# Down weights of the middle experts asked for by ScalarE, behind its copy of the down result, on a queue of their own

## The reference

```
x = x + gt_a * (concat(retention(h), mlstm(h)) @ w_out)
h2 = rms_norm(x, g_ffn) * (1 + sc_f) + sh_f
logits = h2 @ w_router + b_router             # 32 experts, top 4 of each token
expert e:  hu = xe @ w_up[e] + b_up[e]         # w_up[e] is 1024 x 2048
           gate = min(hu[:, :1024], 7);  lin = clip(hu[:, 1024:], -7, 7)
           y = ((lin + 1) * gate * sigmoid(1.702 * gate)) @ w_down[e] + b_down[e]   # 1024 x 1024
x = x + gt_f * (sum over the 4 experts of a token, by its softmax weight)
y = rms_norm(x, g_final)
```

## Time and profile before

| | before |
|---|---|
| median of three runs | 1326.92 us |
| the profiled execution | 1324.58 us, span 1322.8 us |
| TensorE busy (PE) | 1189.2 us, 90% of the span |
| ScalarE busy (ACT) | 176.3 us, 13% |
| read from memory | 459.66 MB, 352 GB/s over the span |
| packets of queue 1 | 461.75 MB, 85.8% of the 16 engines' span |
| packets of queue 10 | 4.37 MB, 1.1% |

### The profile page before, as it was taken

How to read it: one execution, slowest core, us unless ns; L and a number is a source line. 1 busy time by engine, 2 the same in 40 slices (tenths; PEclk the granted TensorE clock), 3 DMA queues, 4 the chain that set the end, 5 groups by cost and what they waited for, 6 DMA issues and landing times.

```text
span 1322.8 us, 23572 instructions
## 1 busy us (share of the span) xinstructions
PE 1189.2 (90%) x8761; PEld 556.1 (42%) x8764; DVE 387.1 (29%) x857; ACT 176.3 (13%) x334; POOL 71.6 (5%) x180
## 2 busy tenths in 40 slices
PE   5999999898989999998999988999877989988996
PEld 4655447645534344443334432444222334333332
DVE  0173215737331221231222121132211221222225
ACT  3002231012101001010111100011110000110101
POOL 1010001323000000000000000000000000000001
PEclk9999999988989999998999998999988999989998
DMA  9934634784569999999999999999999999999992
GB/s 371 358 129 177 225 128 192 223 322 145 235 238 404 396 415 410 422 421 423 421 422 422 422 422 422 422 387 423 423 422 422 422 421 423 420 422 422 423 421 89
DMA packets 80911, 467.22 MB, mean 353 GB/s; under 512 B 8714, under 2 KB 26958, under 8 KB 28778
## 3 DMA queue, kind: packets, MB, share of 16 engines
q1 hardware_dynamic: 78202, 461.75, 85.8%
q10 hardware_dynamic: 2288, 4.37, 1.1%
q0 software_dynamic: 384, 0.59, 0.2%
HBM read 459.66 MB, written 6.42 MB: 352 GB/s over the span
## 4 chain that ended last, share of the span: by engine, by line
PE 65%; DMA 20%; SPq 8%; DVE 3%; issue 3%; POOL 0%; ACT 0%; POOLq 0%; DVEq 0%
PE psum L998 18%; DMA mem<-in_w_up 18%; PE psum L1036 12%; PE psum L1046 8%; SPq L417 7%; PE psum L650 6%; PE psum L965 4%; PE psum L631 3%; PE psum L837 2%; DMA mem<-in_mod_chunks 2%; PE psum L654 2%; PE psum L506 1%; PE psum L758 1%; PE psum L1054 1%; PE psum L1002 1%
## 5 line engine op out<-in xcount | busy, mean ns | idle before, releaser
L998 PE MATMUL psum<-mem 128*32 128x512 f32 (+2 forms) x2432 | 404.3, 626 | 83.8 <-DMA mem<-in_w_up 61.4
L998 PEld LDWEIGHTS psum<-mem 128*32 128x32 f32 (+2 forms) x2432 | 122.2, 122 | 357.5 <-issue 215.8
L1036 PE MATMUL psum<-mem 128*32 128x512 f32 (+3 forms) x1024 | 213.0, 598 | 0.0
L2066 DVE TENSOR_SCALAR mem<-psum 128x256 f32<-128x256 f32 (+3 forms) x32 | 19.2, 601 | 554.8 <-PE psum L1002 554.8
L1046 PE MATMUL psum<-mem 128*128 128x512 f32 (+1 forms) x384 | 152.2, 607 | 2.0 <-issue 1.5
L2087 DVE TENSOR_TENSOR mem<-mem,psum 128x1024 f32<-128x1024 f32 (+1 forms) x96 | 100.3, 1045 | 97.7 <-PE psum L1046 97.7
L1036 PEld LDWEIGHTS psum<-mem 128*32 128x32 f32 (+3 forms) x1024 | 79.6, 128 | 106.2 <-issue 100.0
L965 PEld LDWEIGHTS psum<-mem 128*128 128x128 bf16 x2304 | 77.5, 99 | 20.4 <-issue 20.1
L650 PE MATMUL psum<-mem 128*128 128x512 f32 x192 | 84.2, 595 | 0.0
L965 PE MATMUL psum<-mem 128*128 128x64 bf16 (+1 forms) x2304 | 81.3, 197 | 0.0
L1392 ACT ACTIVATE mem<-mem 128x256 f32<-128x256 f32 (+3 forms) x32 | 17.9, 559 | 465.7 <-DVE mem L2066 465.7
(11 more groups left out here) (275 smaller groups left out, 820.0 us busy)
## 6 DMA issues: line engine op xcount, KB each, us to landing
mem<-in_w_up SPq DMA_DIRECT2D x256, 1024.0 KB, 22.9
mem<-in_w_down SPq DMA_DIRECT2D x128, 1024.0 KB, 17.9
mem<-in_mod_chunks SPq DMA_DIRECT2D x12, 2048.0 KB, 12.2
mem<-in_in_chunks SPq DMA_DIRECT2D x8, 2048.0 KB, 9.8
mem<-in_out_chunks SPq DMA_DIRECT2D x2, 2048.0 KB, 10.0
mem<-in_x_prompt ACTq DMA_DIRECT2D x2, 1024.0 KB, 6.4
mem<-in_state_ret SPq DMA_DIRECT2D x4, 512.0 KB, 8.6
mem<-in_state_mlstm_c SPq DMA_DIRECT2D x4, 512.0 KB, 7.8
```

What stands on the lines that cost most here:

```text
L998: last = pe.matmul(out, xg[:, c, cols], moving, start=(c == 0), stop=False)
L1036: last[c] = pe.matmul(psum[slots * q:slots * q + slots, 6 + u, :], turned, piece_slot(home + c, 2, D)[:, piece % 2, 512 * u:512 * u + 512] ...
```

## The change

SyncE no longer asks for the down pieces of experts 1 to 30. ScalarE does, at the end of its iteration e, for the down pieces of expert e, after it has issued the copy of the down result of expert e-1. It needs no wait of its own for the places, since its copy of the turned activations (L1409) already waits for all four `piece_done`. The down pieces of expert 0 and of the last expert stay with SyncE. The branch for blocks over 128 tokens is changed likewise; it doesn't run with these inputs.

```
-            def load_downs(e, it):
-
-                for c in range(DOWN):
-                    sp.wait_ge(piece_done[UP + c], it)
-                    load_down(e, c)
-
...
             with sp.Fori(2, NE) as e:
                 load_ups(e, e)
-                load_downs(e - 1, e - 1)
             sp.wait_ge(S("counts_ready"), 1)
...
+            def load_downs(e):
+
+                for c in range(DOWN):
+                    src = a["w_down"][0][e, 256 * c:256 * c + 256, :].rearrange("(p h) n -> p h n", h=2)
+                    act.dma_start(piece_slot(UP + c, 2, D), src).then_inc(piece_in[UP + c], 16)
+
...
             with act.Fori(1, NE) as e:
                 expert(0, e, e, count_at(e + 1), count_at(e + 2))
+                with act.If(e < NE - 1):
+                    load_downs(e)
+                with act.Else():
+                    act.nop()
```

More of the change, by code:

```diff
@@ L466, in _ @@
                 with sp.Fori(1, ROUNDS) as r:
-                    load_ups(0, r * NE)
-                    load_downs(NE - 1, r * NE - 1)
-                    with sp.Fori(1, NE) as e:
+                    with sp.Fori(0, NE) as e:
                         load_ups(e, r * NE + e)
-                        load_downs(e - 1, r * NE + e - 1)
                 load_last(NE * ROUNDS)
@@ L1458, in _ @@
                 with act.Fori(1, ROUNDS) as r:
+                    load_downs(NE - 1)
                     copy_gathered(r * (NE + 1), None)
```

## The result

| | before | after |
|---|---|---|
| median | 1327.07 us (4 runs, 1325.17 to 1330.02) | 1361.51 us (4 runs, 1354.69 to 1367.36) |
| ratio, 95% interval | | 1.0255 [1.0212, 1.0298] |
| profiled execution, span | 1324.58, 1322.8 us | 1364.28, 1362.4 us |

The account below looks back on a forecast made before the run. The DMA engines were taken to bound the expert loop. Late asks 22 us plus end order 6 us gave 28 us, which on the profiled 1324.6 us made 1352 us, range 1335 to 1374.

Parts of the forecast that it names:

- SyncE's removed asks 0: Expert loop: SyncE's standing at L422 until the down was done held nothing back, so gain 0.
- ScalarE's four asks 0: End of ScalarE's iteration: four asks take 1.9 us plus a branch, but ScalarE then idles 17.24 us, so 0.
- The heavy downs' lateness, 22 us: Behind the four 96- or 128-slot downs, later asks idle the DMA engines: +7, 12.2 together, +3; bounds 7 and 47 us.
- the even sharing behind its 7.6: Downs at 485 and 721 us: if queues shared evenly beforehand, 16.9 us of work is left, idle 7.6 us.
- The +3 at 899: Heavy down at 899 us: the existing 2.8 us gap grows with a smaller reserve, taken as +3 us.
- The order costs nothing while the DMA engines stay busy: Whole loop: two queues side by side change delivery order but not bytes, so only the end costs time.
- The order at the end, 6 us: Last experts: expert 30's down pieces slip ahead of the last up piece, 5.3 to 7 us; bounds 0 and 9.9.
- everything after 1273.41 moves with the last up piece: Kernel end: expert 31's down is paced by TensorE and copies, not its weights, so the end shifts with that piece.
- Halves: DMA engines: queues 10 and 1 were taken to get half each when both have work; the forecast had 63%.
- The first rival: DMA queues: served in the order of the asks, so only the late asks count, 22 us: 1347; chance 15%.
- the second, less than half for queue 10: Light experts: queue 10 gets clearly less than half, TensorE waits for down pieces, +23, about 1375 us; chance 10%.
- The third (hidden): Downs at 485, 721 and 899 us: the 12-place reserve is enough; within 0.5%, about 1328 us; chance 8%.

Follow-up runs that it names:

- the second profile: The changed kernel run once more, unchanged; median 1359.55 us, ratio 1.0250 to the kernel before.
- late_one_queue: Against the kernel before: all down pieces stay on SyncE's queue 1, but asked for only after ScalarE's copy of the down result; 1338.08 us, ratio 1.0088.
- early_two_queues: Against the changed kernel: ScalarE asks ahead of its two last copies, each piece as its place comes free; 1343.58 us, ratio 1.0129 to the kernel before.

## Why the prediction was right, and where its sizes were off

- *The DMA engines are the bound, and a late or ill-ordered ask costs what they stand idle.* Right: idle time (27.3) and order (6.8) make up all of the loop's 33.9 us.
- *SyncE's removed asks 0, ScalarE's four asks 0.* Right in effect. ScalarE's asks don't wait for its copy: 10.6 us lateness at the first piece of a heavy down and not 11.75.
- *The heavy downs' lateness, 22 us.* In size near, in cause mixed. Idle time grew by 27.3 us in the changed kernel (30.6 in the second profile, 3.0 of them at the start of the loop). By place, less before, it is 8.9 at the first 96-slot down (forecast 7), 6.0 and 6.3 at the next two (6.1 each), and 4.0 behind the up products of the 128-slot expert (3). But late_one_queue, with the lateness alone, has only 8.4, 2.2 and 4.6 at the three downs; the rest comes with the order, of which the forecast for the second and third had a part, the even sharing behind its 7.6. The +3 at 899 is not lateness at all: lateness alone gave +0.5 there, the order alone +7.1. Left out were 4.4 us behind the up products of the 96-slot expert 11 (722 to 730 us), 1.3 behind the 128-slot down, and the 2.6 us ahead of the second heavy down that vanish.
- *"The order costs nothing while the DMA engines stay busy, as the bytes are the same, but it does at the end".* This is where the prediction falls short. They do not stay busy: in early_two_queues less is still to come when the longest step begins, 1.3 up pieces instead of 4.1 beside the same four down pieces. By itself the order cost 9.1 us of idle time; lateness (13.6) and order make 22.7, and the two together 27.3.
- *The order at the end, 6 us.* 6.8 and 6.8 in the two profiles; 18.9 less 12.4 was worked out, 17.4 less 10.6 measured. But "everything after 1273.41 moves with the last up piece" left out that TensorE is idle 1.9 us less once the DMA line is empty, so the term's net is about 5. The end of these two profiles differs by 3.6 us, but 1.7 of that is the busy time, which varies whatever the kernel.
- *Halves.* Right. Between 1040 and 1048 us the two queues share evenly (queue, packets, MB, share of the 16 engines):

```profile
q10 hardware_dynamic: 229, 1.74, 52.3%
q1 hardware_dynamic: 229, 1.62, 48.8%
```

  From 480 to 488 us queue 10 has 2.15 MB of 3.34, and from 1302 to 1310 only 1.40 of 3.39, but this is no unequal sharing: in the first case queue 1, whose next ask is issued at 478.77, moves nothing from 479 to 482, in the second queue 10, asked from 1300.16 on, moves nothing until 1303. From 479 to 482 us, then from 483 to 491, then from 1304 to 1312:

```profile
q10 hardware_dynamic: 172, 1.28, 102.3%
```
```profile
q1 hardware_dynamic: 232, 1.77, 53.2%
q10 hardware_dynamic: 229, 1.61, 48.5%
```
```profile
q10 hardware_dynamic: 225, 1.71, 51.4%
q1 hardware_dynamic: 231, 1.66, 50.0%
```

  The Trainium skill ("DMA: Bandwidth & Descriptors", section "Queues, rings and completion order") has each DMA engine take turns between the queues that have work, a packet at a time. These rows agree: 53.2 against 48.5% and 50.0 against 51.4% of the engines where both have work. The first rival (service in the order of the asks) is out: queue 10 gets its half at once from 1304 us on, and the pieces behind the last up piece would have stayed as they were, 17.4 us and not 10.6. So is the second, less than half for queue 10: TensorE's waits for down pieces came about without it. The third (hidden) and the fourth (faster) are out by the time and by the unchanged 421 to 423 GB/s.
- *The sum.* Loop and end together, 28 us forecast, 30.3 (1012.8 less 982.5) and 33.7 in the two profiles; the medians give 34 and 32. The sum came nearer than its steps did, and that is in part luck: the idle time that the order makes in the middle of the loop was hardly in it, but the lateness was priced above what it costs alone.

## What to carry to other kernels

Where the DMA engines are the bound, count what is still to come at each moment, not what is there: an ask delayed from "this place is free" to "all places are free" costs nearly only where a long step of the compute engine empties the queue: here 8.4, 2.2 and 4.6 us for delays of about 12 us at three such steps, and some 4 us for 26 others together. A second queue adds no bandwidth; it changes the order of delivery, and pieces that are fetched ahead of those wanted first lower the reserve that carries the DMA engines over the next long step, here by 2.8 pieces and 7 us at the longest one, and by 1.4 pieces when only half of them are fetched ahead. One queue in the order of use, with each piece asked for as its place comes free, was the best of the versions run here.

## What was not expected of the hardware

- The part ahead of the loop took 340.1 to 349.6 us in the twelve profiles, whatever the kernel; two profiles alone would have given 9 us of difference that isn't there. The granted clock from 240 to 300 us was 0.91 in the profiles of before and after with the early start and 0.80 in the two others.
- A DMA issue of ScalarE started 0.11 us before the copy that stands ahead of it in the program.
- Two queues that both had work shared the DMA engines by 52 to 48, 48 to 52 and 51 to 49 percent of the bytes (queue 10 first). A stretch of 8 us that takes in 2 us in which one queue moves nothing shows 64 to 36.
- TensorE's pause ahead of the turning of its last expert's weights was 3.47 to 3.65 us in five profiles with full DMA engines, 0.77 to 1.43 in six with idle ones.
- The same 194 products at the end took TensorE 33.1 to 36.2 us from one profile to another.
